# Five early expert rows summed beside TensorE: scaled by ScalarE, added by GpSimd, folded in by VectorE

## What is computed

```
s = einsum('nhid,hikd->nhik', (x @ w_query).reshape(-1, 8, 2, 128), sub_keys)
top_s, top_i = top_k(s, 16)                    # per head, two tables of 128 keys
best_s, pos = top_k(pair sums, 16);  g = softmax(best_s)
act = gelu(einsum('nd,nhkd->nhk', x, u_table[idx])) * g
out = einsum('nhk,nhkd->nd', act, v_table[idx])
```

## Time and profile before

| | before |
|---|---|
| median of three runs | 855.67 us |
| the profiled execution | 852.47 us |
| its span, first to last instruction | 850.7 us |
| what lies around the span | 1.8 us |
| instructions | 10332 |
| busy: TensorE / VectorE / GpSimd / ScalarE | 714.2 / 592.4 / 372.4 / 336.7 us |
| bytes by DMA | 321.7 MB, of these 268.5 MB by the gathers |
| mean granted clock of TensorE | 0.969 of full |

### The profile page before, as it was taken

The page is one execution under the profiler, slowest core; times in us unless marked ns, Lnnn a source line. Parts: engine busy times, 40 slices in busy tenths (PEclk is TensorE's granted clock), DMA queues, the critical chain, the costliest instruction groups (busy, mean ns, idle before and its releaser), DMA issues. The chain is left out here.

```text
span 850.7 us, 10332 instructions
## 1 busy us (share of the span) xinstructions
PE 714.2 (84%) x3385; PEld 354.7 (42%) x3385; DVE 592.4 (70%) x1284; ACT 336.7 (40%) x984; POOL 372.4 (44%) x335
## 2 busy tenths in 40 slices
PE   3899999998969989899878887777877877778784
PEld 0586656645624366567423232223322222222221
DVE  7979613774697668858978766787687568645454
ACT  3413441445374424443344343343334333533331
POOL 3528900343525344355545444555544534444410
PEclk8999999999989999999989999998999999999998
DMA  9966596789989999999999999999999999999991
GB/s 354 411 212 226 208 395 258 269 314 378 413 357 369 421 390 391 421 421 421 421 420 422 421 420 421 421 423 420 422 421 423 420 421 422 421 421 421 422 421 73
DMA packets 50270, 321.74 MB, mean 378 GB/s; under 512 B 9948, under 2 KB 10652, under 8 KB 12200
## 3 DMA queue, kind: packets, MB, share of 16 engines
q0 software_dynamic: 36864, 268.45, 76.7%
q1 hardware_dynamic: 12984, 52.44, 16.1%
q10 hardware_dynamic: 368, 0.18, 0.1%
HBM read 318.77 MB, written 1.23 MB: 376 GB/s over the span
## 5 line engine op out<-in xcount | busy, mean ns | idle before, releaser
L823 PE MATMUL psum<-mem 128*128 128x512 f32 x944 | 468.7, 629 | 103.3 <-ACT mem L1201 102.4
L1478 POOL DMA_INDIRECT mem<-uv_table,small x254 | 301.0, 1185 | 342.3 <-PE psum L823 287.4
L1833 DVE CUSTOM_DVE_ANT_0 mem<-mem,h 128x1024 f32<-128x1024 f32 x254 | 309.9, 1225 | 186.0 <-DMA mem<-uv_table,small 180.2
L823 PEld LDWEIGHTS psum<-mem 128*128 128x128 f32 x944 | 170.8, 196 | 370.9 <-ACT mem L1201 226.6
L1190 ACT ACTIVATE small<-small 128x1 f32<-128x1 f32 x256 | 51.8, 202 | 305.6 <-DVE small L1833 303.0
L1201 ACT ACTIVATE mem<-consts,small 128x128 f32<-128x128 f32 x238 | 95.6, 402 | 7.8
L1195 ACT ACTIVATE small<-small 128x1 f32<-128x1 f32 x256 | 75.4, 294 | 24.6 <-ACT small L1190 1.5
L770 PEld LDWEIGHTS psum<-hT,mem 128*128 128x128 f32 x480 | 58.7, 196 | 14.6 <-issue 10.0
L770 PE MATMUL psum<-hT,mem 128*128 128x128 f32 x480 | 59.4, 280 | 4.2 <-DMA mem<-w_query 4.2
L1393 POOL TENSOR_SCALAR small<-small 128x1 f32<-128x1 f32 (+1 forms) x9 | 5.9, 651 | 87.2 <-DVE small L1863 39.9
L492 PE MATMUL psum<-mem,scol 128*32 128x512 f32 x128 | 21.0, 736 | 15.6 <-DMA mem<-w_mod 15.6
(11 more groups left out here) (225 smaller groups left out, 642.4 us busy)
## 6 DMA issues: line engine op xcount, KB each, us to landing
mem<-w_mod SPq DMA_DIRECT2D x24, 1024.0 KB, 9.1
mem<-w_query SPq DMA_DIRECT2D x8, 1024.0 KB, 9.1
mem<-w_out SPq DMA_DIRECT2D x4, 1024.0 KB, 7.7
mem<-uv_table,small POOLq DMA_INDIRECT x254, 23.9
mem<-w_in_u SPq DMA_DIRECT2D x2, 1024.0 KB, 14.4
mem<-w_in_qkv SPq DMA_DIRECT2D x2, 1008.0 KB, 12.9
mem<-w_ukv SPq DMA_DIRECT2D x1, 1024.0 KB, 8.1
mem<-w_glu SPq DMA_DIRECT2D x1, 1024.0 KB, 4.7
```

Of the source, the lines that this page charges most:

```text
L823: mm = pe.matmul(bank(f"acc_{g}_{half}"), diag[:, pick % DEEP, :], row_of(pick)[:, D + 512 * half:D + 512 * half + 512], start=first, stop ...
L1478: pool.indirect_dma_start(row_of(pick), None, uv_table, bass.IndirectOffsetOnAxis(ap=idx[:, pick:pick + 1] if pick else first_idx, axis=0) ...
L1833: dve.tensor_tensor_reduce(out=row[:, 0:D], in0=row[:, 0:D], in1=h[:, pick // PICKS, :], scale=1.0, scalar=0.0, op0=ALU.mult, op1=ALU.add, ...
```

## The change

Picks 3, 6, 10, 14 and 18 leave `accumulate`. ScalarE, in the place where it scaled the identity matrix (128x128), now scales the second half of the row buffer itself (128x1024): in place, and for pick 3, the first, into the new sum `pooled`. GpSimd adds the scaled row to `pooled`, inside `gather`, just ahead of the gather that takes the row's buffer. For pick 3 there is nothing to add: the gather of pick 8 waits for ScalarE only. After the product of pick 24 VectorE adds `pooled` to `side` once.

```diff
+BY_POOL = [3, 6, 10, 14, 18]
+FOLD = 24
@@
-    return pick + 1 - added_rank(pick)
+    return pick + 1 - added_rank(pick) - pooled_rank(pick)
@@
+        pooled = yb[:, 512:1536]
@@ TensorE
-                if pick not in ADDED:
+                if pick not in ADDED and pick not in BY_POOL:
                     accumulate(pick)
@@ ScalarE, weigh(pick)
                 act.wait_ge(wts_ready, pick + 1)
+                if pick in BY_POOL:
+                    rank = pooled_rank(pick)
+                    row = row_of(pick)[:, D:2 * D]
+                    act.activation(row if rank > 1 else pooled, row, ACT.Copy, scale=wts[:, cut_]).then_inc(row_scaled, 1)
+                    return
@@ GpSimd, gather(pick)
+                elif ROW_BEFORE[pick] in BY_POOL:
+                    add_scaled(ROW_BEFORE[pick])
@@
+            def add_scaled(pick):
+                rank = pooled_rank(pick)
+                pool.wait_ge(row_scaled, rank)
+                if rank > 1:
+                    pool.wait_ge(row_pooled, rank - 2)
+                    pool.tensor_tensor(pooled, row_of(pick)[:, D:2 * D], pooled, ALU.add).then_inc(row_pooled, 1)
+                    pool.wait_ge(row_pooled, rank - 1)
@@ VectorE
+                if pick == FOLD:
+                    dve.wait_ge(row_pooled, len(BY_POOL) - 1)
+                    dve.wait_ge(row_added, added_rank(FOLD))
+                    both = pooled.rearrange("p (a n) -> p a n", a=2)
+                    step(dve.tensor_tensor(side, side, both, ALU.add))
```

More of the change, by code:

```diff
@@ L87, with pooled_rank @@
 ADDED = [2, 5, 9, 13] + list(range(41, 96, 4))
+BY_POOL = [3, 6, 10, 14, 18]
+FOLD = 24
 LATE = 16
 def summed_rank(pick):
-    return pick + 1 - added_rank(pick)
+    return pick + 1 - added_rank(pick) - pooled_rank(pick)
 def added_rank(pick):
     return sum(p <= pick for p in ADDED)
+def pooled_rank(pick):
+    return sum(p <= pick for p in BY_POOL)
 def bank_plan():
@@ L320, in layer @@
         qkv_used, first_ready = sem("qkv_used"), sem("first_ready")
+        row_scaled, row_pooled = sem("row_scaled"), sem("row_pooled")
         ut_in, toep_in = ([sem(f"{n}_in{c}") for c in range(NC)] for n in ("ut", "toep"))
```

## The result

The changed kernel took 861.75 us in the median of five runs (859.96 to 863.92), the kernel before beside it 855.38 us; the ratio is 1.0079, with a 95% interval of 1.0055 to 1.0103. So it is slower by 0.6 to 1.0%: clear of no change, and just inside the 1% that the prediction had called unmeasurable. In a second measurement of the same file the median was 859.12 us beside 855.43, ratio 1.005 (1.003 to 1.007). Forecast were +0.5 us; it was +6.4 and +3.7.

The account below looks back on a forecast made before the run. Up to 226 us the ring of few buffers was the bound, TensorE its slowest link, then VectorE. Pick 20's -0.8 plus the fold's +1.3 gave +0.5 us: 853.0, or 856.2 in terms of the median, range 851.5 to 860.5.

Parts of the forecast that it names:

- Relief and early gathers: Picks 3 to 19: TensorE loses 8.6 us of work; gather 8 goes 3.5 us sooner, gather 11 1.0 us later.
- ScalarE: Scaling a row takes 1.14 us instead of 0.40 for an identity: 0.74 us more for each of five picks.
- The additions' own time: GpSimd's four additions of 128x1024 ahead of gathers: 2.8 us each, hardly under 2.5; no gather can be issued meanwhile.
- what pick 20 wins goes into the end one for one: Picks 20 to 24 keep VectorE busy without a hole, so pick 20's 0.8 us gain reaches the end.
- A product that falls under an addition may take 0.8 us more: VectorE's two-input products beside GpSimd's additions: the shared memory interface slows them, by 0.8 us.
- The list of buffers: Gathers 8 to 19, buffer by buffer: early ones win, additions give most back; pick 19 lands 0.8 us sooner.
- rival 3: TensorE idles more, before 226 us and before pick 25, so its lower clock lasts longer: +9 us, 865; chance 0.05.
- Gather 19: Waits for pick 14's product, weight, scaling and addition, 6.1 us with hand-overs: issued at 215.7, 0.3 us later.
- The issue or the queue decides, I take the middle: Pick 19's landing: 0.3 us later if issue decides, 2.0 sooner if queue decides; middle taken, 0.8 us sooner.
- The fold, +1.3: VectorE's one addition between product 24 and the attention scores' maximum: nothing hides it, so the DMA hole's end moves 1.3 us.
- Rival 2: Additions become the bound, all gathers queue behind them; at 3.9 us each +3.5 us, 859.2; chance 0.22.
- Rival 1: TensorE's relief counts in full, filling the DMA holes before 226 us: 852.4 us, range 850.8 to 854.0; chance 0.27.

Follow-up runs that it names:

- the moved fold: Changed kernel with VectorE's fold of `pooled` moved from behind product 24 to behind product 36: 857.81 us, ratio 1.0035; again 858.02 us, 1.0057.
- the memsets: Changed kernel with each of GpSimd's four additions replaced by three zero fills of the same tile, reading nothing: 858.25 us, ratio 1.0055.
- before again: The unchanged kernel profiled a second time, nothing changed against before: 855.14 us, where its first profiled execution took 852.47.

## Why the prediction was wrong

- **Relief and early gathers: right.** Gather 8 stood 1.24 us behind gather 7, gather 11 at +1.5 us (predicted +1.0), and gather 13 at -1.9 us (predicted -2). From 178.4 to 186.4 us 340 GB/s were moved (above 330 predicted).
- **ScalarE: right.** This row is the scaling of pick 6; 1.1 to 1.2 us were predicted, and the run without it shows no cost at the end.

```profile
188.80 1.15 ACT L1210 ACTIVATE mem<-mem,small 128x1024 f32<-128x1024 f32 x1
```

- **The additions' own time: right, in part by luck.** 2.35 to 3.44 us, 2.84 in the mean, 2.8 taken. An undisturbed one takes 2.35 us, under the floor of 2.5 that the prediction drew; the rest is how much of a VectorE instruction is left at their start. The two errors cancel in the mean.
- **The step that failed: "what pick 20 wins goes into the end one for one", -0.8 us.** Product 20 stood at 232.35, a shift of +3.4 us, where 225 to 227 on the clock of before was predicted; the three other profiles of the same instructions up to there have +1.2, +1.1 and +1.7. From product 20 to 24 the sum puts nothing, and the shift grew to +3.6, +2.7, +3.9 and +1.7, 3.0 in the mean. Without the additions it is -2.0, -1.3 and -2.0: nearly 5 us of product 24 are the additions.
- **What that step left out, first: the wait.** "A product that falls under an addition may take 0.8 us more" had the mechanism and not its size. The 0.8 was read off short pairs as a slowing; it is a wait for the rest of the addition, 1.6 to 2.2 us each in the rows above. And it stands in no step of the forecast, neither for VectorE nor, the other way, for the addition ahead of gather 14, which took 3.44 us instead of 2.8.
- **Second: the later additions.** The list of buffers ends at gather 19. The addition ahead of gather 24, and what late products do to TensorE between picks 15 and 21 (rival 3 below), have no term. How much of the 5 us is the hold of the gathers and how much the wait of VectorE stays open.
- **Gather 19: its chain right, its start wrong.** From product 14 to gather 19 6.1 us were predicted, and 220.71 - 214.60 = 6.11 us were measured; no VectorE instruction of this chain fell under an addition. Gather 19 was still at +2.9 instead of +0.3, as product 14 began at +2.0 instead of -0.6: 0.9 us because gather 14 was issued at +0.35 instead of -0.5, and 1.7 because pick 14 came 8.3 us after its issue (206.30 to 214.60) for 6.7 before. That last part needs no change of the kernel: in the second profile of the unchanged one pick 14 took 8.5 us; the other profiles of the changed kernel and of the moved fold have 5.9, 8.2 and 6.5, and gather 19 at +0.8, +1.8 and +1.4.

```profile
203.69 0.96 POOL L1478 DMA_INDIRECT mem<-uv_table,small  x1 [5.13 <-PE psum L823]
212.18 1.23 DVE L1833 CUSTOM_DVE_ANT_0 mem<-mem,h 128x1024 f32<-128x1024 f32 x1 [3.33 <-DMA mem<-uv_table,small]
```

- **"The issue or the queue decides, I take the middle": wrong.** The halfway point assumed a queue that stays full. It didn't: 358 GB/s against 385. Nor is all of that the gathers', as the first paragraph of the prediction has it: of the 16.19 MB from 184 to 226 us 2.10 are the router's weights (`w_query`).
- **The fold, +1.3: right up to product 31** (1.25 measured), unproven at the end.
- **The base.** The sum was made on an execution of 852.47 us, which the second profile of the same kernel shows to be favourable: it escaped the 2.4 us between products 31 and 32. The correction to the median was made, so this cost the forecast nothing, but it makes each comparison against that profile look worse than the medians.
- **Rival 2 named the right cause; that its 859.2 us fit is luck.** It named the additions as the bound; measured were 859.12 and 861.75. But it asked for additions of 3.9 us and let itself be decided "from additions of about 3.3 us on"; they came to 2.84 in the mean, and it was decided all the same, since VectorE pays as well. Its sum has a slip too: gather 19 waits for two additions in a row, so 1.1 us more for each gives +0.3 + 2.2 + 0.8 = +3.3 us and not +2.2, and the rival's time would be 860.3. That this side would follow from a shared interface, the prediction had said beside it, and had then given it less weight than the rows of small additions.
- **Rival 1 (relief in full, -3.3 us): wrong.** Even without the additions the median was only 1.2 us better, 1.9 with the fold moved as well.
- **Rival 3 (TensorE's clock): there, worth one or two us and not nine.** The prediction had named both places. Before 226 us: the granted clock over picks 8 to 19 was 0.96, 0.88, 0.92 and 0.96 in the four profiles of the changed kernel and the moved fold, 0.92 with the memsets, 0.96 in the kernel without additions and scaling, and 1.00 in both of before and in the six others. Three rows of the second profile of the changed kernel show how it comes in:

```profile
214.46 3.17 DVE L1856 CUSTOM_DVE_ANT_0 mem<-mem,h 128x1024 f32<-128x1024 f32 x1 [2.85 <-DMA mem<-uv_table,small]
218.75 3.78 PE L831 MATMUL psum<-mem 128*128 128x512 f32 x4 [3.38 <-ACT mem L1214]
230.58 0.49 DVE L1811 MAX8 mem<-late 128x8 f32<-128x128 f32 x2 [1.06 <-ACTq L1177]
```

A product stands under an addition, TensorE is idle for 3.38 us and then takes 3.78 us for a pair of 1.88, at the lower level. The router's scores come later by both, VectorE's search waits 1.06 us for them, and the shift grows from +1.2 at product 20 to +2.3 at product 21. In the hole behind pick 25: TensorE waited 4.56 us before pick 25; in the earlier trace rows picks 26 to 31 took 12.26 us.

```profile
252.96 3.78 PE L831 MATMUL psum<-mem 128*128 128x512 f32 x4 [4.56 <-ACT mem L1214]
...
259.00 13.51 PE L831 MATMUL psum<-mem 128*128 128x512 f32 x24 [2.27 <-ACT mem L1214]
```

The granted clock of the last stretch was 0.54 of full, nearly all of it at the lower level of 1.2 GHz, where it had been 0.82. The 24 matmuls took 1.25 us more. But the kernel without additions and with the later fold showed 13.60 us and the second profile of before 13.29, at a clock of 0.58 from 248 to 260 us, so this part isn't the change's doing.

The range reached to 860.5 us. It held the second measurement, and missed the first by 1.25 us.

## What to carry to other kernels

Work given to GpSimd beside a VectorE that reads two SBUF inputs isn't wholly work in parallel: count each GpSimd instruction that reads SBUF as its own time plus, once each way, what is left of the other's instruction. Before anything is put ahead of a gather in the issuing engine's queue, cost the hold by itself (here three memsets were enough to show it) and try the work behind the issue if a scratch is to be had, which was the cheaper of the two here (1.0020 for 1.0050 and 1.0079). Compare one profile with a second of the same kernel before a shift of one or two us is explained: two of the unchanged kernel differed by 3.8 us at one gather. Where an instruction of 1.28 us on VectorE does the same as 1.15 on ScalarE, 2.35 on GpSimd and a fold, look first whether VectorE waits for data anyway: for at least four of the five rows it did.

## What the runs showed of the hardware

**The lock reaches the issue of gathers.** I knew of additions that wait; I hadn't expected that issuing a gather waits as well. Of the 255 issues behind the first in the trace of the kernel before, 120 begin when VectorE runs no instruction with two SBUF inputs, and all of these take 0.93 to 0.95 us, the 30 that begin under another instruction of VectorE too. 135 begin under one with two, and take what is left of it and 0.82 us (the median; all but seven between 0.80 and 0.94). The traces of changed, without additions and before again have the same 0.82. The other way it doesn't hold: 137 products began while an issue was under way, and none took over 1.25 us. It makes a lottery out of the tightest place, gather 32 behind the DMA's hole. In the second profile of before it was issued 0.18 us after a long instruction of VectorE had begun, and stood until that one was done:

```profile
257.12 2.94 POOL L1478 DMA_INDIRECT mem<-uv_table,small  x1 [6.30 <-PE psum L823]
```

```profile
255.56 1.23 DVE L1833 CUSTOM_DVE_ANT_0 mem<-mem,h 128x1024 f32<-128x1024 f32 x1
256.94 2.29 DVE L1690 TENSOR_TENSOR mem<-mem,small 128x2048 f32<-128x2048 f32 x1
```

256.94 + 2.29 - 257.12 + 0.82 = 2.93 us, and 2.94 were measured. In the first profile of the same kernel the issue came just ahead of that instruction:

```profile
255.09 1.38 POOL L1478 DMA_INDIRECT mem<-uv_table,small  x1 [4.62 <-PE psum L823]
```

It took 1.38 us. In the changed kernel the same gather's issue took 2.65 us, and 0.95 in the one without additions. The fourteen profiles fall into two kinds by it. In eight the long instruction (2.29 us) began 0.07 to 0.67 us ahead of this issue, the issue took 2.43 to 3.04 us, and product 32 lost 2.4 to 2.5 us on product 31. In six it began 0.01 to 0.72 us behind, the issue took 0.94 to 1.38 us, and product 32 lost nothing (-0.2 to +0.2). No run forces the order of the two, so this is a rule without exception and not an experiment; but it lies across the kernels, and both kinds occur in before and in fold at 36. So a tenth of a us at one pick goes with 2.4 us at the next. The last gathers of the two profiles with the fold at 36 stood 3.8 us apart: 2.2 us were there by product 31, this step added 2.3, and 0.7 was made up later.

**A memset on GpSimd doesn't take part in it.** One of 128x1024 takes 0.95 us and leaves VectorE's products at 1225 ns.

**Left open:** why pick 14 takes 5.9 to 8.5 us from its issue to its product in profiles of nearly the same kernel, with additions and without, and why gather 52 has 1.4 us more shift than gather 51 in the changed profile.
